# Grouped-query attention with its query tiles in the order latent, context, latent, context

## The chip, the core and the metric

The kernel runs as one program on one core of one Trainium2 chip. The metric is device time in microseconds (us) of that core, the median of several executions. A core has five engines that run their own instruction streams and meet only at semaphores: TensorE (PE: matmuls and transposes, written to PSUM; PEld is its weight load), VectorE (DVE), ScalarE (ACT), GpSimd (POOL) and SyncE (SP, which issues the DMAs here).

## The reference, cut to what matters

The reference is two transformer blocks of depth 2 on 256 latent tokens, the second one with 256 context tokens beside them. The change lies in one mixer of the second block, grouped-query attention with 8 query heads and 2 key heads of 64 columns, which is run once:

```python
k_all = jnp.concatenate([k_ctx, k_lat], axis=1)
v_all = jnp.concatenate([v_ctx, v_lat], axis=1)

def attend(q, k, v):
    s = jnp.einsum("bqhgd,bkhd->bhgqk", q, k).astype(jnp.float32) * ATTN_SCALE
    p = jax.nn.softmax(s, axis=-1).astype(v.dtype)
    return jnp.einsum("bhgqk,bkhd->bqhgd", p, v)

o = lax.map(lambda qb: attend(qb, k_all, v_all), q_blocks)        # latent queries: 512 keys
o_ctx = attend(q_ctx..., k_ctx, v_ctx)                            # context queries: 256 keys
```

A latent query sees all 512 keys, a context query the 256 context keys only.

## The kernel before

The program is a row of phases, with a block of instructions for each engine in each and a meeting of all engines between them: feed-forward and mixer phases of the first block, then those of the second. The change touches one phase, `gqa_attend` (L2155 to L2291), between the projection of queries and keys (`gqa_project`) and the recurrent mixer (`hgrn_phase`).

In it the 8 heads are four **sets** of two heads (`SETS`), and the 512 queries are four **tiles** of 128: tiles 0 and 1 are latent, 2 and 3 context (`TT` is 2, `TILES` is 4). A **unit** is one set with one tile, and `UNITS` (L2168) lists the 16 of them in the order in which every engine takes them. `first(u)` and `keys(u)` give the keys of a unit: 512 for a latent unit (called L below), 256 for a context unit (called C). Before, each set is L, L, C, C.

A unit goes through seven steps:

- scores (PE, L2207): two matmuls, one for each head, into PSUM banks 0 and 1 or 2 and 3, by whether the unit's number is even or odd
- maximum (DVE, L2261): one reduction over the scores of both heads
- exponential (ACT, L2276): two instructions, each with a read of the running sum, into `gqa_e`, which has two halves, by even and odd units
- scaling (DVE, L2251 and L2255): one reciprocal and two multiplications
- turn (PE, L2219): 8 transposes for L, 4 for C, into `TP`, PSUM banks 4 and 5. There is one `TP` for all units
- copy (ACT, L2285): two copies from `TP` to `gqa_pt`, which has two halves
- values (PE, L2231): 8 matmuls for L, 4 for C in the listing of instructions (16 and 8 in the trace, where each counts twice), into bank 6 or 7 by the set; after the last unit of a set ACT copies the bank to `y_T` (L2291)

The queue orders are written out by three loops over u. PE does scores(u), turn(u-2), values(u-3). DVE does maximum(u), scaling(u-1). ACT does exponential(u), copy(u-2), and the copy to `y_T` when unit u-4 was the last of its set. The waits that matter here: scores(u) waits for exponential(u-2); the maximum for its scores; exponential(u) for its maximum and for turn(u-2), since it overwrites that half of `gqa_e`; turn(u) for its scaling and for copy(u-1), since there is one `TP`; copy(u) for turn(u); values(u) for copy(u).

Of the kernel before, what the change touches and what calls it, by code (L numbers as in the profile page):

```python
# [46 lines left out]
TT = S // P  # L47
# [1574 lines left out]
def mixer1_attend(nc, k, m, w, l):  # L1622

    names = ["cs_done", "cs_kept", "c_done", "c_step", "c_exp", "c_zeroed", "c_ready", "ct_done", "ct_kept", "yc_done", "yc_kept", "s_done", "max_ready", "e_ready", "rs_step",
             "t_done", "t_kept", "pv_done", "sum_step", "y_turned", "y_kept", "out_w"]
    UNITS = [(h, tt) for h in range(NH) for tt in (1, 0)]
    NU = len(UNITS)
    BLOCKS = [(g, tt) for g in range(NG) for tt in (1, 0)]
# [3 lines left out]
    with ExitStack() as ctx:  # L1632
# [11 lines left out]
        with phase(nc, names) as (block, s):  # L1644
# [10 lines left out]
            def s_bank(u):  # L1655
                return k.ps[:, u % 3, :].rearrange("p (b t) -> p b t", b=2)

            def t_bank(u):
                return k.ps[:, 3 + u % 2, :].rearrange("p (b c t) -> p b c t", b=2, c=TT)
# [13 lines left out]
            def _(pe):  # L1673
# [29 lines left out]
                def scores(u):  # L1703
                    h, tt = UNITS[u]
                    n = (tt + 1) * P
                    if u >= 3:
                        pe.wait_ge(s["e_ready"], u - 2)
                    pe.matmul(s_bank(u)[:, :, 0:n], m.q_T[:, h, tt * P:(tt + 1) * P], m.k_T[:, h // HPG, :, 0:n], start=True, stop=False,
                              skip_group_check=True)
                    pe.matmul(s_bank(u)[:, :, n - P:n], k.ident_r[:, :], k.causal_r[:, :, :], start=False, stop=True,  # L1710
                              skip_group_check=True).then_inc(s["s_done"], 1)

                def turn(u):
# [3 lines left out]
                    for b in range(2):  # L1717
                        for c in range(UNITS[u][1] + 1):
                            last = pe.transpose(t_bank(u)[:, b, c, :], e[:, u % 3, b, c * P:(c + 1) * P], k.ident[:, :])
                    last.then_inc(s["t_done"], 1)  # L1720

                def values(u):
                    h, tt = UNITS[u]
                    g = h // HPG
                    pe.wait_ge(s["t_kept"], u + 1)
                    if u >= 2:
                        pe.wait_ge(s["sum_step"], 2 * (u - 2) + 2)
                    for b, v in enumerate((m.v_slc, m.v_win)):
                        for c in range(tt + 1):
                            last = pe.matmul(o_bank(u, b), pt[:, u % 2, b, c, :], v[:, c, g * HD:(g + 1) * HD], start=(c == 0), stop=(c == tt),  # L1730
                                             skip_group_check=True)
                    last.then_inc(s["pv_done"], 1)
# [29 lines left out]
            def _(dve):  # L1762
# [19 lines left out]
                def greatest(u):  # L1782
                    dve.wait_ge(s["s_done"], u + 1)
                    dve.tensor_reduce(nmax[:, u, :], s_bank(u)[:, :, 0:(UNITS[u][1] + 1) * P], AX.X, ALU.max, negate=True).then_inc(s["max_ready"], 1)

# [369 lines left out]
def gqa_attend(nc, k, b, m, ahead):  # L2155
# [9 lines left out]
    NP = GQ // GKV // 2  # L2165
    TILES = 2 * TT
    SETS = [(j, g) for j in range(NP) for g in range(GKV)]
    UNITS = [(i, tt) for i in range(len(SETS)) for tt in range(TILES)]  # L2168
    NU = len(UNITS)
    with ExitStack() as ctx:  # L2170
        def sb(name, shape):
# [1112 lines left out]
def second_block(nc, k, w):  # L3284
    with ExitStack() as ctx:
# [31 lines left out]
        with ExitStack() as outer:  # L3317
            hgrn, hgrn_ahead = hgrn_buffers(nc, outer, w)
            with ExitStack() as inner:
                m, gqa_ahead = gqa_buffers(nc, inner, w)  # L3320
                prenorm_phase(nc, k, b, 0, [0, 1], gqa_ahead, first=True)
                gqa_project(nc, k, b, m, hgrn)
                gqa_attend(nc, k, b, m, hgrn_ahead)
            rows = out_rows("even_w_out_2")
            hgrn_phase(nc, k, b, w, hgrn, [(out_raw[:, n, :], rows[n]) for n in range(OUT_SLOTS)])
# [144 lines left out]
```

## Time and profile before

| | us |
|---|---|
| median of 3 executions | 2429.6 (2428.79 to 2431.62) |
| the profiled execution, its own time | 2431.38 |
| its span, first to last instruction | 2429.6 |
| `gqa_attend` in it, from the first scores to the last copy to `y_T` | 1209.3 to 1263.6, 54.3 |
| PE, DVE, ACT busy in the whole span | 2258.6, 1442.9, 1141.8 |

The profile is one execution. Its page gives the busy time of each engine over the span, the same in 40 slices, and the costliest groups of instructions. The trace behind it can be asked for a stretch: the busy time of each engine and the clock that TensorE was granted, who waited for whom, and the instructions of an engine in order of time. The phase of the change is 2.2% of the span, so the page's totals hardly show it and the stretch has to be read by itself.

### The profile page before, as it was taken

The page shows a single profiled execution, that of the slowest core. Times are in us where ns is not written, and L with a number is a line of the kernel's source. Part 1 is how long each engine was busy: PE and PEld are TensorE (multiplying, and loading weights), DVE is VectorE, ACT ScalarE, POOL GpSimd, SP SyncE. Part 2 cuts the span into 40 slices and gives each one's busy share as a digit, 9 for nine tenths or more (in the row PEclk, how much of TensorE's full clock was granted, in tenths as well). Part 3 has the DMA queues.
Part 4 walks back from the last instruction along what each step waited for, and adds up shares of the span by engine and source line. Part 5 has one row for each costly group of instructions (what it writes and reads, how often), then busy time and mean ns, then how long its engine had stood idle before and what let it go on. Part 6 is the DMA issues. An engine that isn't in the chain of part 4 may idle for free. (4 is left out here: it accounts for less than half of the span.)

```text
span 2429.6 us, 37637 instructions
## 1 busy us (share of the span) xinstructions
PE 2258.6 (93%) x14312; PEld 1865.2 (77%) x14312; DVE 1442.9 (59%) x2398; ACT 1141.8 (47%) x1979; POOL 81.1 (3%) x117
## 2 busy tenths in 40 slices
PE   8999989999999989996879997889999989988998
PEld 7877878888787878875558886678888778877886
DVE  6664457667656357666446675375555554447886
ACT  4443454444444455444366664353433444445554
POOL 0000000000000000000002222000000000000000
PEclk9999999999999999998999998989999979998999
DMA  8886317876886435772112110153333343305662
GB/s 266 272 250 206 107 53 228 264 234 176 257 257 207 107 105 180 262 251 89 36 32 63 45 63 2 35 147 117 117 113 112 122 121 87 96 1 160 189 196 87
DMA packets 389938, 346.83 MB, mean 143 GB/s; under 512 B 24388, under 2 KB 353464, under 8 KB 389304
## 3 DMA queue, kind: packets, MB, share of 16 engines
q1 hardware_dynamic: 380029, 294.62, 41.0%
q10 hardware_dynamic: 9787, 50.52, 5.3%
q8 instruction: 84, 1.38, 0.2%
q14 instruction: 38, 0.31, 0.0%
HBM read 344.05 MB, written 1.05 MB: 142 GB/s over the span
## 5 line engine op out<-in xcount | busy, mean ns | idle before, releaser
L710 PE MATMUL ps<-x_hi_lo,gu_hi 128*128 128x512 f32 x1680 | 423.7, 394 | 1.3 <-DVE gu_sum L900 1.3
L710 PEld LDWEIGHTS ps<-x_hi_lo,gu_hi 128*128 128x128 f32 x1680 | 305.7, 188 | 80.2 <-issue 18.1
L900 DVE TENSOR_REDUCE gu_sum<-ps 128x256 f32<-128x512 f32 x220 | 150.6, 690 | 244.0 <-PE ps L712 240.6
L803 ACT ACTIVATE gu_hi<-w_gu 128x1024 fp32r<-128x1024 f32 x220 | 228.9, 1054 | 120.9 <-DMA w_gu<-in_ffn_w_up 46.8
L883 DVE TENSOR_TENSOR gu_lo<-w_gu,gu_hi 128x1024 fp32r<-128x1024 f32 x220 | 260.9, 1220 | 17.7 <-ACT gu_hi L803 17.5
L712 PEld LDWEIGHTS ps<-x_hi_lo,gu_lo 128*128 128x128 f32 x1680 | 228.8, 190 | 16.7
L712 PE MATMUL ps<-x_hi_lo,gu_lo 128*128 128x256 f32 x1680 | 233.8, 282 | 0.0
L739 PE MATMUL ps<-dn_hi,h_hi 128*128 128x512 f32 x440 | 173.3, 394 | 3.9 <-DVE h_lo L927 3.9
L739 PE MATMUL ps<-dn_lo,h_hi 128*128 128x512 f32 x440 | 172.5, 392 | 0.0
L739 PE MATMUL ps<-dn_hi,h_lo 128*128 128x512 f32 x440 | 171.3, 389 | 0.0
L819 ACT ACTIVATE silu<-gu_sum 128x256 f32<-128x256 f32 x88 | 36.7, 417 | 263.1 <-DVE gu_sum L900 262.5
L891 DVE TENSOR_TENSOR dn_lo<-w_dn,dn_hi 128x1024 fp32r<-128x1024 f32 x110 | 134.6, 1223 | 15.2 <-ACT dn_hi L807 10.7
L807 ACT ACTIVATE dn_hi<-w_dn 128x1024 fp32r<-128x1024 f32 x110 | 115.6, 1056 | 54.8 <-PE ps L739 54.8
L1063 PE MATMUL ps<-both_x_hi,gu_hi 128*128 128x512 f32 x320 | 124.5, 389 | 0.0
L1063 PE MATMUL ps<-both_x_lo,gu_hi 128*128 128x512 f32 x320 | 124.5, 389 | 0.0
L1063 PE MATMUL ps<-both_x_hi,gu_lo 128*128 128x512 f32 x320 | 124.5, 389 | 0.0
L1227 DVE SCALAR_TENSOR_TENSOR conv<-ps,par,conv 128x510 f32<-128x510 f32 x44 | 30.9, 745 | 128.9 <-ACT conv L1167 128.9
L739 PEld LDWEIGHTS ps<-dn_hi,h_hi 128*128 128x128 f32 x440 | 83.0, 189 | 19.2 <-issue 4.8
L739 PEld LDWEIGHTS ps<-dn_hi,h_lo 128*128 128x128 f32 x440 | 82.7, 188 | 18.1
L739 PEld LDWEIGHTS ps<-dn_lo,h_hi 128*128 128x128 f32 x440 | 83.1, 189 | 13.3
L1167 ACT ACTIVATE conv<-ps,par 128x512 f32<-128x512 f32 x44 | 31.8, 774 | 130.4 <-PE ps L1063 120.9
L1063 PEld LDWEIGHTS ps<-both_x_hi,gu_lo 128*128 128x128 f32 x320 | 60.1, 188 | 12.6
(465 smaller groups left out, 4768.4 us busy)
## 6 DMA issues: line engine op xcount, KB each, us to landing
w_gu<-in_ffn_w_up SPq DMA_DIRECT2D x176, 512.0 KB, 6.2
w_dn<-in_ffn_w_down SPq DMA_DIRECT2D x132, 512.0 KB, 3.6
w_mod<-in_w_mod ACTq DMA_DIRECT2D x64, 768.0 KB, 7.4
w_gu<-in_ffn_w_gate SPq DMA_DIRECT2D x88, 512.0 KB, 5.1
odd_w<-in_odd_w_qkv SPq DMA_DIRECT2D x24, 512.0 KB, 5.2
w_gu<-in_ffn_w_down SPq DMA_DIRECT2D x11, 1024.0 KB, 5.0
hgrn_w<-in_even_w_in SPq DMA_DIRECT2D x20, 512.0 KB, 3.9
wo<-in_w_out SPq DMA_DIRECT2D x2, 4096.0 KB, 13.0
```

Source lines behind the costliest of these rows:

```text
L710: pe.matmul(gu(a), gu_hi[n][:, a, f, :], x_both[:, f, :, :], start=(f == 0), stop=False, skip_group_check=True)
L712: last = pe.matmul(gu(a)[:, 0, :], gu_lo[n][:, a, f, :], x_hi[:, f, :], start=False, stop=(f == FT - 1), skip_group_check=True)
L739: last = pe.matmul(k.ps[:, 2 * tt + c, :], h[n][:, tt * P:(tt + 1) * P], wt[n][:, c * BANK:(c + 1) * BANK], start=(first and p == 0), stop ...
L803: act.activation(gu_hi[n][:, a, :, :], wgu[n][:, a, :, :], ACT.Copy).then_inc(s["w_hi"], 1)
L807: act.activation(dn_hi[n][:, :], wdn[n][:, :], ACT.Copy).then_inc(s["w_hi"], 1)
L819: act.activation(sil[n][:, :], c[n][:, 0, :], ACT.Silu).then_inc(s["act_done"], 1)
L883: last = dve.tensor_tensor(gu_lo[n][:, a, :, :], wgu[n][:, a, :, :], gu_hi[n][:, a, :, :].bitcast(F32), ALU.subtract)
L891: dve.tensor_tensor(dn_lo[n][:, :], wdn[n][:, :], dn_hi[n][:, :].bitcast(F32), ALU.subtract).then_inc(s["dn_split"], 1)
L900: dve.reduce_sum(c[n][:, a, :], gu(a).rearrange("p h t -> p t h"), AX.X).then_inc(s["c_ready"], 1)
L1063: last = pe.matmul(gu(n, a), wt[n][:, a, f, :], x[:, f, :], start=(f == 0 and p == 0), stop=(f == FT - 1 and p == 2))
L1167: act.activation(cv[n][:, a, :, :].rearrange("p s t -> p (s t)"), gu(n, a), ACT.Identity, bias=conv.bias(t, a), scale=conv.tap(1, t, a)).t ...
L1227: dve.scalar_tensor_tensor(cv[n][:, a, :, 1:S], streams(n, a)[:, :, 0:S - 1], conv.tap(0, t, a), cv[n][:, a, :, 1:S], ALU.mult, ALU.add).t ...
```

## The change

The list of units is written in another order. Within each set the tiles come as 0, 2, 1, 3, which is L, C, L, C in place of L, L, C, C. The loops, waits and buffers are the same text, and the number of instructions of each kind is the same; which units share a half of `gqa_e`, `gqa_pt` or the score banks follows from the new numbers (even units are now all L, odd ones all C). The first tile of a set is still tile 0 and the last still tile 3.

```diff
     SETS = [(j, g) for j in range(NP) for g in range(GKV)]
-    UNITS = [(i, tt) for i in range(len(SETS)) for tt in range(TILES)]
+    UNITS = [(i, tt) for i in range(len(SETS)) for tt in (0, TT, 1, TT + 1)]
     NU = len(UNITS)
```

On PE, in the second set (turn is L2219, values L2231, scores L2207; 512 or x8 is L, 256 or x4 is C). Before:

```order
1714 L2219 MATMUL ps<-ident,gqa_e 128x128 x8
1715 L2231 MATMUL ps<-gqa_pt,gqa_v 64x128 x4
1716 L2207 MATMUL ps<-gqa_k_T,gqa_q_T 128x256 x2
1717 L2219 MATMUL ps<-ident,gqa_e 128x128 x8
1718 L2231 MATMUL ps<-gqa_pt,gqa_v 64x128 x8
1719 L2207 MATMUL ps<-gqa_k_T,gqa_q_T 128x512 x2
1720 L2219 MATMUL ps<-ident,gqa_e 128x128 x4
1721 L2231 MATMUL ps<-gqa_pt,gqa_v 64x128 x8
1722 L2207 MATMUL ps<-gqa_k_T,gqa_q_T 128x512 x2
1723 L2219 MATMUL ps<-ident,gqa_e 128x128 x4
```

And after:

```order
1718 L2219 MATMUL ps<-ident,gqa_e 128x128 x4
1719 L2231 MATMUL ps<-gqa_pt,gqa_v 64x128 x8
1720 L2207 MATMUL ps<-gqa_k_T,gqa_q_T 128x512 x2
1721 L2219 MATMUL ps<-ident,gqa_e 128x128 x8
1722 L2231 MATMUL ps<-gqa_pt,gqa_v 64x128 x4
1723 L2207 MATMUL ps<-gqa_k_T,gqa_q_T 128x256 x2
```

Before, a round of turn, values and scores has four makes in four rounds. After, there are two makes that alternate: a C turn with L values and L scores, then an L turn with C values and C scores.

On ACT, one set from its first exponential (exponential is L2276, copy L2285). Before:

```order
592 L2276 ACTIVATE gqa_e,gqa_sums<-ps,gqa_max 128x512 x2
593 L2285 ACTIVATE gqa_pt<-ps 128x256 x2
594 L2276 ACTIVATE gqa_e,gqa_sums<-ps,gqa_max 128x512 x2
595 L2285 ACTIVATE gqa_pt<-ps 128x256 x2
596 L2276 ACTIVATE gqa_e,gqa_sums<-ps,gqa_max 128x256 x2
597 L2285 ACTIVATE gqa_pt<-ps 128x512 x2
```

And after:

```order
593 L2276 ACTIVATE gqa_e,gqa_sums<-ps,gqa_max 128x512 x2
594 L2285 ACTIVATE gqa_pt<-ps 128x512 x2
595 L2276 ACTIVATE gqa_e,gqa_sums<-ps,gqa_max 128x256 x2
596 L2285 ACTIVATE gqa_pt<-ps 128x256 x2
597 L2276 ACTIVATE gqa_e,gqa_sums<-ps,gqa_max 128x512 x2
```

Before, an exponential of one kind was always followed by a copy of the other kind; after, by a copy of its own kind.

## Rows read from the trace of the kernel before

**Rows 1.** Busy time by stretch: us, then each engine, PEclk, DMA share, GB/s.

```profile
1222.23:1234.98 12.75, 9.99 (x92) 6.30 (x90) 7.11 (x17) 8.46 (x25) 0.00 (x0) 1.00 0.00 1
```

**Rows 2.** Waits in the phase: total us, times, longest us.

```profile
PE ps L2219 <- ACT gqa_pt L2285: 9.5, 13, 1.2
...
ACT gqa_e L2276 <- PE ps L2219: 10.2, 8, 1.3
...
ACT gqa_e L2276 <- DVE gqa_max L2261: 6.0, 7, 1.3
```

**Rows 3.** PE in order of time: start us, busy us, instruction, idle before and releaser.

```profile
1217.77 1.06 PE L2219 MATMUL ps<-ident,gqa_e 128*128 128x128 f32 x8 [1.60 <-DVE gqa_e L2255]
1218.77 1.09 PE L2231 MATMUL ps<-gqa_pt,gqa_v 128*64 128x128 f32 x16
1219.79 1.13 PE L2207 MATMUL ps<-gqa_k_T,gqa_q_T 64*128 64x512 f32 x4
1221.07 0.63 PE L2219 MATMUL ps<-ident,gqa_e 128*128 128x128 f32 x4 [0.15 <-ACT gqa_pt L2285]
1221.63 1.09 PE L2231 MATMUL ps<-gqa_pt,gqa_v 128*64 128x128 f32 x16
...
1224.37 0.63 PE L2219 MATMUL ps<-ident,gqa_e 128*128 128x128 f32 x4 [0.58 <-ACT gqa_pt L2285]
1224.92 0.66 PE L2231 MATMUL ps<-gqa_pt,gqa_v 128*64 128x128 f32 x8
1225.51 0.70 PE L2207 MATMUL ps<-gqa_k_T,gqa_q_T 64*128 64x256 f32 x4
1227.23 1.06 PE L2219 MATMUL ps<-ident,gqa_e 128*128 128x128 f32 x8 [1.01 <-ACT gqa_pt L2285]
```

**Rows 4.** ACT in order of time, the same stretch: exponentials and copies.

```profile
1218.93 0.47 ACT L2276 ACTIVATE gqa_e<-ps,gqa_max 128x256 f32<-128x256 f32 x1 [1.30 <-PE ps L2219]
...
1219.85 1.08 ACT L2285 ACTIVATE gqa_pt<-ps 128x512 f32<-128x512 f32 x2
1222.23 0.69 ACT L2276 ACTIVATE gqa_e<-ps,gqa_max 128x512 f32<-128x512 f32 x1 [1.30 <-DVE gqa_max L2261]
...
1223.57 0.65 ACT L2285 ACTIVATE gqa_pt<-ps 128x256 f32<-128x256 f32 x2
1225.09 0.69 ACT L2276 ACTIVATE gqa_e<-ps,gqa_max 128x512 f32<-128x512 f32 x1 [0.87 <-DVE gqa_max L2261]
...
1228.39 0.47 ACT L2276 ACTIVATE gqa_e<-ps,gqa_max 128x256 f32<-128x256 f32 x1 [1.31 <-PE ps L2219]
```

**Rows 5.** DVE in order of time, the same stretch: maxima of an L and a C unit.

```profile
1220.97 1.23 DVE L2261 TENSOR_REDUCE gqa_max<-ps 128x2 f32<-128x1024 f32 x1 [3.34 <-PE ps L2207]
...
1226.26 0.69 DVE L2261 TENSOR_REDUCE gqa_max<-ps 128x2 f32<-128x512 f32 x1 [0.22 <-PE ps L2207]
```

**Rows 6.** The start of the phase on PE, DVE and ACT, in order of time.

```profile
1213.33 0.70 PE L2207 MATMUL ps<-gqa_k_T,gqa_q_T 64*128 64x256 f32 x4 [1.95 <-ACT gqa_e L2276]
...
1213.51 0.88 DVE L2255 TENSOR_SCALAR gqa_e<-gqa_e,gqa_rs 128x512 f32<-128x512 f32 x2
...
1215.63 0.47 ACT L2276 ACTIVATE gqa_e<-ps,gqa_max 128x256 f32<-128x256 f32 x1 [1.03 <-PE ps L2219]
```

**Rows 7.** The end of the phase on PE and ACT, in order of time.

```profile
1259.34 0.63 PE L2219 MATMUL ps<-ident,gqa_e 128*128 128x128 f32 x4 [1.21 <-ACT gqa_pt L2285]
...
1260.01 0.66 ACT L2285 ACTIVATE gqa_pt<-ps 128x256 f32<-128x256 f32 x2 [0.32 <-PE ps L2219]
...
1262.33 0.66 PE L2231 MATMUL ps<-gqa_pt,gqa_v 128*64 128x128 f32 x8 [0.16 <-ACT gqa_pt L2285]
...
1263.03 0.60 ACT L2291 ACTIVATE y_T<-ps 128x512 f32<-128x512 f32 x1 [0.76 <-PE ps L2231]
```

**Rows 8.** Busy time by stretch, two stretches of 2 us, as in rows 1.

```profile
1216.00:1218.00 2.00, 0.40 (x4) 0.26 (x3) 1.38 (x4) 1.63 (x6) 0.00 (x0) 1.00 0.11 30
...
1268.00:1270.00 2.00, 2.00 (x6) 1.60 (x5) 0.00 (x0) 0.00 (x0) 0.00 (x0) 0.50 1.00 289
```

## Prediction

> **What bounds the kernel now.** The change touches 54.3 us of 2431.38, so I read the phase by itself. First the busy times of its second set [rows 1]: in 12.75 us PE is busy 9.99, ACT 8.46, DVE 7.11, at the full clock (2.4 GHz) and with almost no DMA. No engine is full, so waits bound it. Then the waits [rows 2]: turns on PE wait for copies on ACT (9.5 us), exponentials on ACT for turns (10.2 us) and, in other rounds, for maxima (6.0 us). Two chains are at work, and the rows in order of time give their terms, each from the start of one step to the start of the next:
>
> - The **turn chain** goes round the one TP buffer: turn(u-2), exponential(u), copy(u-2), turn(u-1). Turn to exponential is 1218.93 - 1217.77 = 1.16 for an L turn [rows 3, 4]. For a C turn no exponential shows it here. The turn is busy 0.63, and the L turn's gap behind its busy time (1.16 - 1.06) adds 0.10: 0.73. The nearest row that does show what follows a C turn has 0.67 [rows 7]. Exponential to copy is 1.34 for L (1222.23 to 1223.57) and 0.92 for C; copy to turn is 1.22 for L (1219.85 to 1221.07) and 0.80 for C [rows 3, 4].
> - The **score chain** runs through PE's queue, since scores(u+1) stand behind turn(u-2) and values(u-3), and the exponential needs its maximum. An L turn is followed by values after 1.00, a C turn after 0.56; L values by scores after 1.02, C values after 0.59; L scores by their maximum after 1.18, C after 0.75 [rows 3, 5]; an L maximum by its exponential after 1.26 [rows 4, 5].
>
> Before, the turn chain sums over a set to 12.3 us: steps of 2.87 (1.34 + 0.80 + 0.73), 3.30, 3.30 and 2.87. The set takes 12.75 [rows 1]. The missing 0.42 is where a set begins: exponential 4 at 1222.23 waited for its maximum, and 1.00 + 1.02 + 1.18 + 1.26 = 4.46 from the turn at 1217.77 is just that, while the turn chain would have let it go at 1221.07 + 0.73 = 1221.80. The second L unit, 1225.09, is a tie: 1221.07 + 0.56 + 1.02 + 1.18 + 1.26 = 1225.09 against 1222.23 + 2.87 = 1225.10. In the C rounds the turn chain rules, as the row at 1228.39 says.
>
> **What the change does.** No instruction is added or dropped, no DMA moves and SP and POOL have the same queues, so that part is nothing. The edit shifts which L and C steps stand beside each other.
>
> Turn chain after. A round is exponential + copy of one kind and a turn of the other: 1.34 + 1.22 + 0.73 = 3.29 and 0.92 + 0.80 + 1.16 = 2.88. A pair is 6.17, a set 12.34, the same as before. By this chain alone the order gives nothing.
>
> Score chain after. L scores now always stand behind a C turn and L values. Let a C turn start at 0. Its exponential (C) starts at 0.73. L values start at 0.56, L scores at 1.58, the L maximum at 2.76, the L exponential at 4.02. The turn chain would allow it at 0.73 + 2.88 = 3.61, or a little later: the L turn waits behind the L scores on PE until about 2.7, and ends in time for an exponential at 3.9. So the maximum is last, by 0.1 to 0.4, in every L round. From there the L copy follows at 5.36 and the next C turn at 6.58. The loop C turn, L values, L scores, L maximum, L exponential, L copy closes on itself: **6.58 us a pair, 13.16 a set**, against 12.75. Before, this chain took 0.42 once in a set; now it takes 0.41 twice, because the context units that used to come between give it no room to catch up. DVE doesn't add to it: it is free long before an L maximum (its C scaling goes behind the maximum, at about 3.9 to 4.7, and the C turn wants it at 6.58).
>
> **The sum.** Start: exponential 2 is now L. Its scores start at 1213.33, the maximum at +1.18, the exponential at +1.26: 1215.77, against 1215.63 [rows 6]; the scaling ahead of that maximum ends at 1214.39, in time. That is +0.14. From exponential 2 to exponential 14 are six pairs: 6 x 6.58 = 39.48, so 1255.25. Tail, from exponential 14 (L): L exponential and copy 2.56, C turn 0.73, C exponential and copy 1.72, L turn to copy 1.11 (0.67 [rows 7] and the longer turn, 0.44), L copy 1.22, C turn 0.56, L values 1.02, last C values to the copy to y_T 0.70 (1262.33 to 1263.03 [rows 7]): 9.62, so 1264.87 against 1263.03. The sum is **+1.8 us**: about 0.1 at the start, 1.2 in the pairs, 0.5 at the end, where an L unit is now last but one with nothing beside it. All of it passes on, since hgrn_phase begins when the engines meet. The profiled execution would be 2431.38 + 1.8 = 2433.2; its time is 0.07% above the median of the runs, so the median becomes 2429.6 + 1.8 = 2431.4. What is uncertain: the C turn's 0.73 could be 0.67, which leaves the score loop as it is. If the L scores were ready earlier by anything up to 0.41 a pair, the pairs give back up to 2.5, which is the first rival. If PE's queue is tighter than I read, say the scores start 0.1 later, it is +0.6 over six pairs.
>
> **Rivals.** *Only the one TP buffer counts.* If the score chain hides behind the turn chain, a pair is 6.17 and the phase ends near 1264.87 - 2.5 = 1262.4, 0.6 before today's: 2429.0. For it: the margin by which the maximum is last is 0.1 to 0.4, and the rows have a tie at 1225.09. Against it: the 4.46 and the 4.02 fit two starts to 0.01. The Trainium skill (Perfetto Trace Analysis, Optimizing Tensor Performance) says that independent matmul groups should rotate through different PSUM banks so that their evacuation overlaps; by that rule the single TP is what bounds here and no order of units can matter, and the trace agrees for the C rounds but not for the exponential at 1222.23.
>
> *TensorE's clock falls in the phase: slower.* PE will idle some 1.6 us in each pair (from the end of C scores at 4.9 to 6.58), and the score loop now runs through PE three times a pair (0.56 + 1.02 + 1.18 = 2.76). At half clock (1.2 GHz) these at most double: +2.8 a pair, +17 over six, 2448. It decides the sign beyond doubt from two pairs at half clock. Against it: the stretch from 1216 to 1218 has PE busy 0.40 of 2.00 and still the full clock, and a steady pair will be busy about 4.9 of 6.58, no less than that; the half clock shows at 1268 to 1270 [rows 8], behind the pause between this phase and the next, which stays.
>
> *A pause moves.* The half-clock stretch after the phase [rows 8] may start earlier or later against the work or be missed. Two us at half clock do the work of one, so that is some 1 to 2 us either way (an estimate, as the stretch may be longer than the row), inside the range.
>
> *Faster for real*, by over 4.9 us, would need the pairs near 5.8, below the turn chain's sum. Nothing in the rows allows that unless exponential and turn overlap better than these rows show.
>
> **How the numbers follow.** A measurement of this kernel can tell about 0.2%, 4.9 us, from no change. Score loop, +1.8: 0.66. TP buffer alone, -0.6: 0.24. Clock falls, +3 to +17: 0.06. Something faster than the chains: 0.04, of which half passes 4.9 us. So faster 0.02, same 0.93, slower 0.05. Predicted 2431.4. The range takes both likely cases and the scatter of the runs shown (2428.79 to 2431.62): 2427.5 to 2435.5.
>
> **What would show it.** In the profile after: L exponentials wait for their maximum and C exponentials for the turn, in every pair; exponentials of L units 6.58 apart, sets 13.16; PE idle once a pair for about 1.6 us before a C turn; the last copy to y_T 1.8 us later in the phase. Wrong if L exponentials wait for the turn and are 6.17 apart (first rival), or if the granted clock shows 0.50 inside the phase.

## The result, and the profile after

The changed kernel takes 2438.55 us (2433.97 to 2438.71, 7 executions), the kernel before 2430.09 us (2428.33 to 2431.98, 7 executions, the three of the prediction among them). The ratio is 1.0029, with a 95% interval of 1.0020 to 1.0039: slower, by some 7 us by the ratio (the medians are 8.5 apart). The prediction said 2431.4, at most 2435.5, and no change that can be measured. It was wrong.

Each profile of the kernel in the same three parts, the phase of the change (from the first scores to the end of the last copy to `y_T`), the recurrent phase behind it, and all that is behind the phase: us, busy time of PE, PEld, DVE, ACT, POOL, then the granted TensorE clock, DMA share, GB/s. Of the kernel before:

```profile
1209.32:1263.63 54.31, 40.03 (x353) 25.34 (x352) 28.47 (x64) 35.94 (x102) 0.00 (x0) 1.00 0.11 33
1266.28:1595.65 329.37, 289.16 (x3169) 249.79 (x3169) 190.09 (x337) 181.62 (x331) 52.14 (x64) 0.93 0.17 52
1263.63:2429.61 1165.98, 1077.65 (x7285) 909.93 (x7285) 695.15 (x1115) 572.54 (x975) 52.23 (x65) 0.95 0.33 99
```

And of the changed kernel:

```profile
1205.73:1264.67 58.94, 42.71 (x353) 27.00 (x352) 28.56 (x64) 36.00 (x102) 0.00 (x0) 0.94 0.11 31
1267.32:1599.90 332.58, 292.62 (x3169) 253.33 (x3169) 189.69 (x335) 181.54 (x331) 52.16 (x64) 0.92 0.17 52
1264.67:2432.16 1167.49, 1080.67 (x7285) 913.25 (x7285) 695.77 (x1115) 572.76 (x975) 52.26 (x65) 0.95 0.33 99
```

The phase is 4.6 us longer and not 1.8, and its clock is 0.94, which means some 7 of its 59 us at half clock, where before had none. The recurrent phase, whose code is the same, takes 3.2 us more, of which later phases give a part back: all behind the phase is 1.5 longer. TensorE's own busy time in it rises by 3.5 us (289.16 to 292.62) with the same 3169 instructions, so it is the clock that differs and not a wait. This execution began the phase 3.6 us earlier than before's, by the clock it got in the part ahead (0.98 against 0.97), where the two programs are the same; that differs between executions, and it hides more than half of the loss in the spans (2429.6 and 2432.2). The sum that can be compared is from the first scores to the end: 1220.3 before, 1226.4 after.

Where the clock is full, the phase is what the prediction said. ACT in order of time (start, busy us, instruction, idle before and releaser), three latent exponentials in a row with the context ones between:

```profile
1241.43 0.69 ACT L2276 ACTIVATE gqa_e<-ps,gqa_max 128x512 f32<-128x512 f32 x1 [1.72 <-DVE gqa_max L2261]
...
1244.72 0.47 ACT L2276 ACTIVATE gqa_e<-ps,gqa_max 128x256 f32<-128x256 f32 x1 [0.87 <-PE ps L2219]
...
1248.01 0.69 ACT L2276 ACTIVATE gqa_e<-ps,gqa_max 128x512 f32<-128x512 f32 x1 [1.24 <-DVE gqa_max L2261]
...
1251.31 0.47 ACT L2276 ACTIVATE gqa_e<-ps,gqa_max 128x256 f32<-128x256 f32 x1 [0.87 <-PE ps L2219]
...
1254.60 0.69 ACT L2276 ACTIVATE gqa_e<-ps,gqa_max 128x512 f32<-128x512 f32 x1 [1.72 <-DVE gqa_max L2261]
```

A latent exponential waits for its maximum in every pair at the full clock, a context one for the turn, and latent ones are 6.58 and 6.59 us apart. In the waits of the phase this answers to [rows 2]: total us, times, longest us.

```profile
PE ps L2219 <- ACT gqa_pt L2285: 11.1, 8, 1.6
ACT gqa_e L2276 <- DVE gqa_max L2261: 11.0, 7, 2.6
ACT gqa_e L2276 <- PE ps L2219: 9.5, 8, 3.1
```

The wait for the maximum went from 6.0 to 11.0 us. Elsewhere the clock is not full. The busy times of two stretches and of one clean pair behind them:

```profile
1215.80:1219.20 3.40, 3.40 (x17) 1.57 (x14) 0.46 (x1) 1.17 (x6) 0.00 (x0) 0.50 0.02 5
...
1229.60:1232.90 3.30, 3.30 (x21) 2.20 (x21) 0.00 (x0) 2.06 (x7) 0.00 (x0) 0.50 0.00 0
...
1241.43:1248.01 6.58, 4.96 (x48) 3.15 (x46) 3.55 (x9) 4.48 (x13) 0.00 (x0) 1.00 0.00 1
```

PE in order of time in the first of them; turn, values and scores of a pair, and the turn behind them:

```profile
1214.67 0.63 PE L2219 MATMUL ps<-ident,gqa_e 128*128 128x128 f32 x4 [2.15 <-DVE gqa_e L2255]
1215.23 1.45 PE L2231 MATMUL ps<-gqa_pt,gqa_v 128*64 128x128 f32 x16
1216.61 2.08 PE L2207 MATMUL ps<-gqa_k_T,gqa_q_T 64*128 64x512 f32 x4
1218.62 1.37 PE L2219 MATMUL ps<-ident,gqa_e 128*128 128x128 f32 x8
```

Values took 1.38 us to the scores and not 1.02, the scores were busy 2.08 and not 1.13 [rows 3]. The C turn, the values and the scores stand in the score loop, and here the L turn behind them (busy 1.37 and not 1.06) ended, by the profile, a little later than the maximum: the latent exponential at 1220.09 is the one that waited for a turn. The pair around them took 7.99 us (latent exponentials at 1212.10 and 1220.09) and not 6.58, 1.4 more. The pair around the other stretch took 8.17 (1226.67 to 1234.84), 1.6 more.

### The profile page after: what moved, and what is told of

The parts are those of the page before. It is cut to its first block and busy times, and to the rows that moved or that the text cites. A ratio compares the mean times of both kernels' runs of the same rounds, so it can differ in the third digit from the quotient of the medians.

```text
span 2432.2 us, 37637 instructions
## 1 busy us (share of the span) xinstructions
PE 2260.1 (93%) x14312; PEld 1865.4 (77%) x14312; DVE 1443.1 (59%) x2398; ACT 1142.5 (47%) x1979; POOL 80.8 (3%) x117
## 3 DMA queue, kind: packets, MB, share of 16 engines
q8 instruction: 84, 1.38, 0.2%
## 5 line engine op out<-in xcount | busy, mean ns | idle before, releaser
L803 ACT ACTIVATE gu_hi<-w_gu 128x1024 fp32r<-128x1024 f32 x220 | 229.2, 1055 | 119.8 <-DVE gu_sum L900 48.4
L1063 PEld LDWEIGHTS ps<-both_x_lo,gu_hi 128*128 128x128 f32 x320 | 60.1, 188 | 12.6
```

Of the source, the lines that this page charges most:

```text
L803: act.activation(gu_hi[n][:, a, :, :], wgu[n][:, a, :, :], ACT.Copy).then_inc(s["w_hi"], 1)
L1063: last = pe.matmul(gu(n, a), wt[n][:, a, f, :], x[:, f, :], start=(f == 0 and p == 0), stop=(f == FT - 1 and p == 2))
```

## The experiments

Two questions were open: why the clock falls in the phase, and why the time behind the phase changes. In all tables and texts below, "from the first scores" is the time from the first scores to the end of the program in the profiled execution, since the part ahead of them, the same program in all kernels here, took from 1202.0 to 1210.6 us in the profiles.

**The changed kernel again.** No edit.

> The changed kernel once more, unchanged. In the profile of the changed kernel the phase gqa_attend took 58.9 us against 54.3, of which the score loop explains 1.9 and two stretches at half clock inside the phase some 2.9; yet the median is 7 us up and not 4.6. Theory A (the clock falls inside the phase, in a number of stretches that differs between executions): the phase again takes 57 to 63 us, has one to four stretches at a granted clock near 0.5 while before has none, and what is left over outside the phase is under 1 us; 2434 to 2439 in all. Theory B (the clock inside the phase is chance, as it is everywhere): the phase takes about 56.2 us at the full clock, and the missing 5 us lie in other phases. L exponentials are 6.58 us apart wherever the clock is full, by both.

Measured: 2438.07 us (2436.22 to 2439.4, 5 executions) against 2429.89 of before, ratio 1.0036 (1.0022 to 1.0050).

```profile
1207.95:1266.87 58.92, 42.70 (x353) 27.00 (x352) 28.57 (x64) 35.94 (x102) 0.00 (x0) 0.94 0.10 31
1269.53:1602.13 332.60, 292.70 (x3168) 253.47 (x3169) 189.67 (x335) 181.28 (x331) 53.01 (x64) 0.92 0.17 52
```

The phase is the same to 0.02 us, with the same share at half clock, and so is the recurrent phase. So the clock in the phase is no chance, as theory A says. But theory A also had a number of stretches that differs between executions, and here it is the same, and less than 1 us outside the phase, where the recurrent phase alone has 3.2. It is half right.

**Before again.** No edit; it was run with the last ones and stands here for comparison.

> The kernel before once more, as the second profile of it. The phase takes 54.3 us with no half clock, the recurrent phase 329 to 330, and from the first scores to the end 1220 us, by all theories. If the phase shows stretches at half clock here, the comparison of the first two profiles was luck.

Measured: 2429.6 us (2426.86 to 2431.94, 11 executions), ratio 0.9999 (0.9990 to 1.0008).

```profile
1207.74:1262.02 54.28, 39.97 (x353) 25.27 (x352) 28.47 (x64) 35.99 (x102) 0.00 (x0) 1.00 0.11 33
1264.67:1593.90 329.23, 288.96 (x3169) 249.59 (x3169) 190.13 (x338) 181.63 (x331) 52.10 (x64) 0.93 0.17 52
```

As expected: no half clock in the phase, and 1219.9 from the first scores.

**The changed order with TensorE kept busier.** The value products of each context unit are done three times; the same numbers are written thrice.

```diff
-                    for c in range(n):
+                    for c in list(range(n)) * (1 if tt < TT else 3):
```

> The changed order, and TensorE does the value products of every context unit three times over (the same result is written thrice), 16 more small matmuls a unit, about 1.2 us in the pause that TensorE has in each pair. Nothing waits for them: context scores get ready 1.2 us later, at 5.4 of 6.58 us, and their exponential wants them at 7.3. Theory A: with TensorE busier the clock stays full, the phase takes 56.2 us, and the time is the kernel before + 1.9 = 2432, some 5 us under the changed kernel. Theory B: the work is hidden and the time is that of the changed kernel, +7. If the extra work were on the path, it would be slower than the changed kernel by up to 8 x 1.2 = 9 us.

Measured: 2433.93 us (2430.77 to 2435.87, 11 executions), 4 under the changed kernel, ratio to before 1.0020 (1.0011 to 1.0029). The phase:

```profile
1204.67:1263.03 58.36, 48.07 (x481) 32.96 (x480) 28.56 (x64) 35.95 (x102) 0.00 (x0) 0.97 0.10 31
```

One stretch at half clock was left, at 1214.8 us, ahead of the first extra work. The phase takes 58.4 us where 56.2 was expected. The extra work wasn't all hidden: behind the last units nothing covers it (a fault of the experiment, which the control shows too).

**The control: the same in the order of before.** The same edit in the kernel before.

> The control to the run above: the order of before, with the value products of every context unit three times over. Here they stand ahead of scores of context units, whose exponentials have 1.4 us to spare. Both theories: the time of before within 1 us, since no stretch at half clock is there to be taken away. If it is faster than before by more than 1 us, then executions of before had stretches at half clock in this phase too, which its profile doesn't show.

Measured: 2433.57 us (2430.68 to 2436.68, 11 executions), ratio 1.0015 (1.0006 to 1.0024).

```profile
1208.54:1264.17 55.63, 46.74 (x481) 32.29 (x480) 28.47 (x64) 35.94 (x102) 0.00 (x0) 1.00 0.12 33
1266.83:1599.38 332.55, 292.66 (x3168) 253.46 (x3168) 189.72 (x335) 181.30 (x331) 53.02 (x64) 0.92 0.17 52
```

Both theories missed it. The phase is 1.3 us longer by the uncovered work at its end and has no half clock, but the recurrent phase takes 332.6 as behind the changed kernel, and the kernel loses some 3.6 us. So the 3.2 us there don't need the changed order. That they come with the time at which the phase ends is the guess that the delays below test.

**Pauses filled, with nothing on the path.** The changed order, the extra value products in the first three sets only, and 12 transposes that nobody reads ahead of the second turn, into a bank that is free then.

```diff
-                    for c in range(n):
+                    for c in list(range(n)) * (1 if tt < TT or i == len(SETS) - 1 else 3):
...
+                    if u == 3:
+                        for n in range(12):
+                            pe.transpose(k.ps[:, 7, n % 4 * P:(n % 4 + 1) * P], k.x_T[:, 0, 0:P], k.ident[:, :])
                     if 2 <= u < NU + 2:
                         turn(u - 2)
```

> The changed order, with TensorE's pauses filled where nothing waits for it: the value products of context units of the first three sets three times over (not in the last set, where they stood on the path in the run before), and 12 idle transposes ahead of the second turn, where the one stretch at half clock was left. Theory A: no stretch at half clock in the phase, which takes 56.2 to 56.6 us against 58.9 of the changed kernel. The time by the rows is then 2.5 us under the changed kernel by the phase alone; with what the end of the phase does to the phases behind it, 2431 to 2436. If the clock still falls in the phase, theory A names the wrong cause.

Measured: 2433.03 us (2428.63 to 2434.56, 11 executions), 5 under the changed kernel, ratio to before 1.0010 (1.0001 to 1.0019).

```profile
1209.38:1265.31 55.93, 46.24 (x461) 31.85 (x460) 28.56 (x64) 35.94 (x102) 0.00 (x0) 1.00 0.11 33
1267.96:1598.41 330.45, 290.65 (x3168) 250.94 (x3168) 189.71 (x336) 181.63 (x331) 52.14 (x64) 0.92 0.17 52
```

With TensorE busy 46.24 us and not 42.71 the phase has the full clock throughout and takes 55.93 us: 3.0 less than the changed kernel, though TensorE does more. That is the price of the half clock in the phase. Against before's 54.31 it leaves 1.6 for the order itself, which the prediction had at 1.8. Theory A holds for the phase.

Up to the first extra value products this kernel and the one with TensorE kept busier differ by the 12 transposes alone. The second turn, first without them and then with them:

```profile
1213.60 0.63 PE L2219 MATMUL ps<-ident,gqa_e 128*128 128x128 f32 x4 [2.15 <-DVE gqa_e L2255]
...
1218.31 0.63 PE L2219 MATMUL ps<-ident,gqa_e 128*128 128x128 f32 x4 [0.69 <-DVE gqa_e L2258]
```

The pause ahead of it goes from 2.15 to 0.69 us, and the stretch at half clock that began 1.2 us after it is gone. In the pairs the extra products shrink the pause from 1.63 to 0.75 us.

**The phase made to end later.** The order of before, with three or six copies on ScalarE, to buffers that nobody reads, ahead of the last copy to `y_T`.

```diff
...
+                        for n in range(3 if i == len(SETS) - 1 else 0):
+                            act.activation(slots[n], O(i), ACT.Copy)
                         act.activation(b.y_T[:, j + g * NP, :], O(i), ACT.Copy).then_inc(s["o_used"], 1)
```

> The order of before, with three copies of 128x512 on ScalarE (to buffers nobody reads) ahead of the last copy to y_T, so that the phase ends 1.6 us later and nothing else in it changes. In two profiles of the changed kernel the recurrent phase behind this one took 332.6 us against 329.4 before, though its code is the same, and in the control run (phase 1.3 us longer) it took 332.6 too; in the run with the scores first (phase 1.35 shorter) 330.3. Theory C: the stretches at half clock begin at times that don't move with the work, so a later end of the phase changes which work they hit. Then this kernel pays more than its 1.6 us: the recurrent phase takes 332 to 333 us, and the time is 3 to 6 us above before. Theory D (nothing behind the phase depends on when it ends): + 1.6 us, 2431.5.

> The same with six copies: the phase ends 3.3 us later. Theory C: the work meets the clock's steps about where it met them before, the recurrent phase again takes 329 to 330 us, and the time is 3.3 us above before, 2433.2, perhaps no more than with three copies. Theory D: + 3.3 as well, and the recurrent phase unchanged in this run and in the one with three copies.

Measured: 2432.88 us (2426.71 to 2435.6, 11 executions), ratio 1.0011 (1.0002 to 1.0020), with three copies; 2434.43 us (2430.21 to 2435.83, 11 executions), ratio 1.0017 (1.0008 to 1.0027), with six. Phase and recurrent phase, with three copies:

```profile
1208.87:1264.62 55.75, 40.00 (x353) 25.32 (x352) 28.46 (x64) 37.41 (x105) 0.00 (x0) 1.00 0.12 36
1267.28:1599.87 332.59, 292.71 (x3169) 253.46 (x3169) 189.59 (x335) 181.38 (x331) 53.02 (x64) 0.92 0.17 52
```

With six:

```profile
1206.38:1263.59 57.21, 39.97 (x353) 25.26 (x352) 28.47 (x64) 38.92 (x108) 0.00 (x0) 1.00 0.10 32
1266.24:1595.71 329.47, 288.78 (x3168) 249.40 (x3168) 189.84 (x337) 181.82 (x331) 52.16 (x64) 0.93 0.17 52
```

A delay of 1.4 us (55.75 - 54.3) makes the recurrent phase 3.3 us longer, one of 2.9 us leaves it as it was. From the first scores they take 1223.25 and 1223.30 us, both 3.1 or 3.2 over the mean of before's two profiles, 1220.1. Theory D falls, theory C holds in the traces. In the medians, where the part ahead adds its scatter of several us, the two are 1.5 us apart; the intervals overlap. With three copies the median is 2.7 us over before's, a little under the 3 to 6 expected.

That it is the clock, the traces say: in the recurrent phase TensorE stood at half clock for 48.2 and 48.4 us in before's two profiles, 56.1 with three copies, in the control and in the changed kernel (56.2 in its fourth profile), and 46.2 with six copies. One of the stretches that the recurrent phases of 332.6 us have and the others lack begins 98.8 us behind the first scores of the changed kernel. A piece of it, and then the same time behind the first scores in before:

```profile
1304.60:1307.90 3.30, 3.30 (x10) 2.53 (x9) 3.30 (x5) 1.13 (x1) 1.22 (x1) 0.50 0.00 0
...
1308.10:1311.40 3.30, 3.30 (x19) 2.52 (x18) 2.82 (x7) 2.43 (x5) 1.50 (x2) 1.00 0.43 126
```

The end of the phase is not a simple dial, though: with filled pauses the phase was 0.18 us longer than with three copies (55.93 and 55.75), and the recurrent phase took 330.45 and not 332.59.

**The same delay behind the changed phase.** The changed order and the three copies.

> The changed order with the three copies on ScalarE ahead of the last copy to y_T, 1.5 us more. Theory C (later phases meet the clock's steps at other places, and the time behind the phase moves in steps): from the first scores to the end the seven profiles so far sum to 1219.8 to 1220.3, 1223.1 to 1223.3 and 1226.4 us, so a delay is either nearly free or costs some 3. The changed kernel's recurrent phase stands at its slowest, 332.6; 1.5 us later it should take about 330.4, and the time should be that of the changed kernel within 1 us, 2438. Theory D (delays add up): 1.5 us above the changed kernel, 2439.6.

Measured: 2435.76 us (2432.61 to 2438.14, 7 executions), ratio to before 1.0024 (1.0012 to 1.0035).

```profile
1209.70:1270.12 60.42, 42.71 (x353) 27.06 (x352) 28.56 (x64) 37.48 (x105) 0.00 (x0) 0.94 0.12 31
1272.77:1602.43 329.66, 288.80 (x3169) 249.33 (x3169) 189.87 (x337) 181.85 (x331) 52.08 (x64) 0.93 0.17 52
```

The phase is 1.5 us longer than the changed kernel's, the recurrent phase 2.9 shorter, and from the first scores it takes 1226.6. The kernel with 1.5 us more in it is not slower, which only theory C allows. The time expected by it, 2438 within 1, was still 2.2 too high. The list of sums in the expectation leaves out the 1224.3 of the kernel with TensorE kept busier.

**The scores ahead of the values.** On TensorE turn(u-2), scores(u+1), values(u-3), first in the order of before, then in the changed one.

```diff
-                for u in range(NU + 3):
-                    if u < NU:
-                        scores(u)
-                    if 2 <= u < NU + 2:
+                scores(0)
+                scores(1)
+                scores(2)
+                for u in range(2, NU + 3):
+                    if u < NU + 2:
                         turn(u - 2)
+                    if u + 1 < NU:
+                        scores(u + 1)
```

> The order of before, but on TensorE the scores of the next unit come ahead of the value products: turn(u-2), scores(u+1), values(u-3) in place of values, scores. If the score chain costs what I worked out (0.42 us where each set begins), only the turn chain is left: sets of 12.34 us in place of 12.75, exponentials of latent units that wait for the turn and not for their maximum, and the phase 1.2 to 1.4 us shorter: 2428.8. If the one TP buffer is all that counts, as the first rival had it, no change. By theory A the clock stays full.

> The changed order with turn(u-2), scores(u+1), values(u-3) on TensorE. If the score chain is what made a pair 6.58, exponentials of latent units are now 6.17 apart at the full clock and wait for the turn; the phase then takes 53.7 us, or up to 3 more if the clock falls in it. TensorE's pause shrinks from 1.63 to 1.2 us a pair, so by theory A there should be fewer stretches at half clock than the two of the changed kernel. If the pair stays at 6.58, my chain was wrong and something else set it.

Measured: 2430.15 us (2423.82 to 2432.48, 11 executions), ratio 0.9999 (0.9990 to 1.0008), in the order of before; 2433.27 us (2426.34 to 2435.63, 11 executions), ratio 1.0012 (1.0003 to 1.0021), in the changed one. Waits of the first (a few lines were added, so the exponential is L2279 and the maximum L2264 here), and its phase:

```profile
ACT gqa_e L2279 <- PE ps L2219: 14.4, 14, 1.3
...
ACT gqa_e L2279 <- DVE gqa_max L2264: 0.4, 1, 0.4
```

```profile
1210.61:1263.57 52.96, 39.97 (x353) 25.27 (x352) 28.75 (x64) 35.94 (x102) 0.00 (x0) 1.00 0.11 34
1266.22:1596.49 330.27, 289.58 (x3168) 250.13 (x3168) 189.82 (x337) 181.53 (x331) 52.03 (x64) 0.93 0.17 52
```

The wait for the maximum went from 6.0 to 0.4 us and the phase is 1.35 shorter, as worked out: the score chain is real and priced right. The gain doesn't reach the end: the recurrent phase takes 0.9 more, and from the first scores the kernel takes 1219.8, 0.3 under before's mean. In the changed order latent exponentials came 6.40 us apart and not 6.17:

```profile
1229.18 0.69 ACT L2279 ACTIVATE gqa_e<-ps,gqa_max 128x512 f32<-128x512 f32 x1 [1.05 <-PE ps L2219]
...
1235.58 0.69 ACT L2279 ACTIVATE gqa_e<-ps,gqa_max 128x512 f32<-128x512 f32 x1 [1.54 <-PE ps L2219]
```

Its waits in the phase, total us, times, longest us:

```profile
PE ps L2219 <- DVE gqa_e L2258: 10.8, 7, 2.2
```

The miss of 0.2 us a pair is a chain that the prediction had no term for: turns now wait for the scaling on VectorE. One stretch at half clock was left in this phase (56.44 us in all), where two had been.

**Two transpose buffers.** The changed order, outputs of all sets in bank 6, context units turned into bank 7, and the turn waits for the copy two units back; once as it is and once with the scores ahead of the values.

```diff
-            TP = k.ps[:, 4:6, :]
+            def TP(u):
+                return k.ps[:, 4:6, :] if u % 2 == 0 else k.ps[:, 7, :].rearrange("p (h n) -> p h n", h=2)
...
-                return k.ps[:, 6 + i % 2, :]
+                return k.ps[:, 6, :]
...
-                    if u:
-                        pe.wait_ge(s["t_ready"], u)
-                    else:
+                    if u >= 2:
+                        pe.wait_ge(s["t_ready"], u - 1)
+                    elif u == 0:
```

> The changed order with two transpose buffers: latent units (even) turn into PSUM banks 4 and 5, context units (odd) into bank 7, which is had by keeping the outputs of all sets in bank 6; the copy to y_T goes ahead of the copy of turned scores, and the values of a set's first unit wait for it. A turn then waits for the copy two units back and not for the last one, so the loop turn, exponential, copy, turn is open. What remains a pair is ScalarE's work, 1.34 + 0.92 + 1.08 + 0.66 + gaps, 4.1, or TensorE's, 4.9 to 5.3: sets of 10 to 11 us in place of 13.16, and 48 to 51 us in place of 58.9 for the phase, some 4 to 6 us under before. If the score chain (maximum behind scores behind values) still rules, the pair stays at about 6 us.

> Two transpose buffers and the scores first, L C L C. In the run with two buffers a pair took 5.9 us at full clock where it was free of a set's seam, with latent exponentials waiting for their maximum (score chain), and 10.2 us of the phase were at half clock. With the scores ahead of the values a pair should take 5.0 to 5.5, so the phase 48 to 52 us at full clock; each stretch at half clock costs 1.4. The time from the first scores to the end should be one step (3 us) under before's, 2427, if no more than two stretches fall in it.

Measured: 2434.18 us (2428.63 to 2436.44, 11 executions), ratio 1.0015 (1.0005 to 1.0025), with two buffers alone; **2423.8 us** (2422.33 to 2426.34, 11 executions), ratio 0.9975 (0.9966 to 0.9984), with both. The phase with two buffers alone:

```profile
1210.61:1268.93 58.32, 44.30 (x353) 28.15 (x352) 28.56 (x64) 35.18 (x102) 0.00 (x0) 0.91 0.10 31
```

```profile
ACT gqa_e L2277 <- DVE gqa_max L2262: 10.2, 6, 2.1
```

With both:

```profile
1210.49:1258.28 47.79, 39.60 (x353) 25.42 (x352) 29.12 (x64) 35.23 (x102) 0.00 (x0) 1.00 0.13 38
```

Two buffers alone bought 0.6 us of the phase. Away from a set's first values the pair fell from 6.58 to 5.93 us, which is the case of about 6 us that the expectation named for a score chain that still rules: latent exponentials (L2277 here) waited 10.2 us for their maxima. But the clock is 0.91 (10 us at half clock), and the single output bank brings a wait that the changed kernel didn't have, so this isn't a pure test of the one TP buffer:

```profile
PE ps L2232 <- ACT y_T L2284: 7.3, 3, 2.4
```

With the scores first as well the phase takes 47.8 us at the full clock, 6.5 under before, with pairs of 4.9 and 6.2 us in turn where 5.0 to 5.5 was expected, and the kernel beats both others. From the first scores it takes 1214.1, so 6.0 of the 6.5 pass on; the 2427 expected had only one step of 3. The 48 to 51 us expected for two buffers alone failed (58.3); the 48 to 52 for both was missed by 0.2.

**Two more profiles of the changed kernel.** No edit.

> The changed kernel, one more look. The two profiles of it have two stretches at half clock in the phase (6.83 us), 58.9 us for the phase and 1226.4 us from the first scores to the end, 6.3 above before's two profiles, while the medians are 7 to 8 us apart. If other executions have three or more stretches in the phase, the phase here takes 60.4 us or more and the sum from the first scores is near 1229. If not, 58.9 and 1226.4 again, and the missing 1 to 2 us lie ahead of the phase, where the program is the same and the profiles so far range from 1202.0 to 1210.6 us.

> The changed kernel, as in the look before: 58.9 us for the phase and 1226.4 from the first scores if all executions are alike from there on, 60.4 or more and near 1229 if some lose more at half clock.

Measured: 2439.79 and 2439.24 us, with 2430.38 for before beside them, one execution each. Phase and all behind it, of the first:

```profile
1210.27:1269.20 58.93, 42.69 (x353) 27.00 (x352) 28.57 (x64) 36.00 (x102) 0.00 (x0) 0.94 0.10 31
...
1269.20:2438.01 1168.81, 1082.22 (x7285) 914.38 (x7285) 695.77 (x1115) 572.74 (x976) 52.24 (x65) 0.94 0.33 99
```

The phase is the same a third and fourth time (58.94 in the second). Both take 1.3 us more behind it than the first two profiles, nearly all in the last 38 us of the program, and 1227.7 and 1227.8 from the first scores. So four profiles of the changed kernel have 1226.4, 1226.5, 1227.7 and 1227.8, two of before 1220.3 and 1219.9: 7.0 us on the mean, against a loss of 7.0 and 8.7 us by the ratios of the two measurements (1.0029, 1.0036). No more stretches in the phase are needed for it. The expectation had both outcomes, and neither was quite met: the rest was behind the phase, not in it or ahead of it.

## Why the prediction was wrong, point by point

- **The turn chain and the score chain: right.** The pair of 6.58 us is measured at 6.58 and 6.59, with the maximum last in latent rounds and the turn in context rounds. With the clock full the phase costs 1.6 us (55.93 - 54.31) where the sum said 1.8. Taking the score chain away from the order of before gave 1.35 where 1.2 to 1.4 was expected. TensorE's pause of about 1.6 us a pair and its busy time of 4.9 in 6.58 were right as well (the turns' longest wait for copies is 1.6 in the changed phase's waits, and the clean pair is busy 4.96).
- **The first rival, one TP buffer alone: not what happened.** It would have ended 0.6 under before. The experiments with two buffers fit: opening the TP loop alone gains 0.6 us of the changed kernel's phase (58.9 to 58.3, though half clock and a new wait eat part of it), opening both chains 11.1 (to 47.8).
- **"TensorE's clock falls in the phase": the step that failed first.** It got 6 in 100 and was called slower by 3 to 17 us; it cost 3.0 in the phase, in all four profiles. The argument against it was one stretch of 2 us with PE busy 0.40 and the clock full [rows 8]. That row shows that a pause once went unpunished, not that pauses do. It then held the steady pair's 4.9 of 6.58 against that stretch, where the steady set of before was the thing to compare: its longest pause is 1.0 us where after's is 1.6, and it is busy 9.99 of 12.75 [rows 1], 78%, after 4.96 of 6.58, 75%. The share alone tells little, since half of that set, from 1222.23 to 1228.39, is busy 4.57 of 6.16, 74%, at the full clock. Nor is a pause enough: before had pauses of 1.95 and 1.60 us at its start [rows 3, 6], and the changed kernel four of 1.6 us from 1237 on, all with the full clock behind them. By the Trainium skill (TensorE: Matmul & The Clock Gate, Part 1) the clock follows how busy the engine has lately been, on a beat that runs by itself whatever the kernel does. The trace agrees with the first half: more work in the pauses brought the clock back to 1.00 and the phase down by 3.0 us. Whether the beat is independent of the kernel no run here shows by itself.
- **"All of it passes on": the step that failed second.** The sum took what the phase loses as what the kernel loses. From the first scores to the end thirteen of the sixteen profiles fell into three groups, though phases within a group differ by up to 2.7 us: 1219.8 to 1220.3 (before twice, scores first), 1223.1 to 1223.3 (the control, both delays, filled pauses, two buffers), and 1226.4 to 1227.8 (the changed kernel, and with the delay). The other three have 1224.3 (TensorE kept busier), 1224.6 (changed order, scores first) and 1214.1 (two buffers and scores first). A delay of 1.4 us cost 3.1 there, one of 2.9 the same, 1.35 us gained in the phase brought 0.3, and 1.5 us more in the changed kernel cost nothing. The mechanism is the granted clock again: the phases behind have pauses of their own and get half clock in places that depend on when they start, so the recurrent phase takes 329.1 to 330.5 us or 331.9 to 332.7 with the same instructions. The prediction had this under "a pause moves", for one stretch, worth 1 to 2 us either way; it is worth 3.3 in the recurrent phase and a net 1.7 to 3.1 behind the phase.
- **The sum as it should have been**: order 1.6, half clock in the phase 3.0, behind the phase 1.7 to 3.1 (1167.5 to 1168.9 against 1165.8, the mean of before's two). Together 6.3 to 7.7, measured 7.0 and 8.7 by the ratios.
- **The range** left the clock out: its upper end takes the likely cases and the scatter only. 1.8 us of chain alone would have stayed inside it, which the kernel with filled pauses shows (2433.03).

What stays open: why the two stretches fall where they do. Filling the pauses takes them away and scores ahead of values takes one away, while two buffers alone bring more. Open too is how the time behind the phase follows from when the phase ends; the delays show two points of it. No run varied the pause by itself in small steps, so no rule for when the clock falls is claimed, and the shares and pauses above are what these kernels had, not limits.

## What to carry to other kernels

When a reorder leaves TensorE with one longer pause a round in place of several short ones, price the half clock as a likely term and not as a rare one, and compare the longest steady pause before and after, since work in the pause can be cheaper than the pause. A gain or loss of a few us in one phase of a long kernel may pass on in full, hardly, or more than once over (6.0 of 6.5 us, 0.3 of 1.35, 3.1 of 1.4); judge an edit from a common point of the program to its end, in more than one profile. And find every chain that closes within a few tenths of the one that rules: on the changed order each of two fixes alone left the kernel 3 to 4 us slower than before, and both together made it some 6 us faster.

## What the runs showed of the hardware that was not expected

The same 7285 TensorE instructions behind the phase took 1164.7 to 1168.9 us in sixteen profiles, by where the granted clock fell to 0.50 (117 to 132 us of them in all); the part ahead of it, 1202.0 to 1210.6 us. A delay of 1.4 us and one of 2.9 us at the same place gave the same time to the end within 0.1 us (1223.25 and 1223.30). And the stretches at half clock in the changed phase came at the same instructions in all four profiles, with the phase at 58.92 to 58.94 us each time, so what looks like noise of the clock is here largely set by the program. The traces show why that can be: in all sixteen profiles a stretch at half clock ends within 0.2 us of the phase's first scores, however late these come, and in the changed kernel the next two begin 10.1 and 23.7 to 23.8 us behind them each time. What puts the two in step was not tested.
